# A hybrid decoder trunk on one core: more of the recurrence's small products as 64x64 quadrants, and the finishing norm one level later

## The reference

```python
kk = heads(k * k_k)
kk = kk / maximum(sqrt(sum(kk * kk, -1)), 1e-12)      # the key norm
k = k * (1.0 + (a - 1.0) * k_a)
def step(S, inp):
    sa = einsum('bhij,bhj->bhi', S, -kk_t)
    S = (S * w_t[:, :, None, :] + sa[..., :, None] * (kk_t * a_t)[:, :, None, :]
         + v_t[..., :, None] * k_t[..., None, :])
    return S, einsum('bhij,bhj->bhi', S, r_t)
y = (y - mean(y)) * rsqrt(var(y) + eps)               # the finishing norm, per head
y = y * ln_g + ln_b
bonus = sum(heads(r * k * r_k), -1) * heads(v)
return (y + bonus) * g
```

## Time and profile before

| | |
|---|---|
| median of 3 runs | 883.57 us (883.24 to 883.83) |
| profiled execution | 883.92 us, its span 882.1 us |
| mean granted TensorE clock | 0.977 |
| PE / PEld busy | 828.9 us (94%) / 555.5 us |
| DVE / ACT / POOL busy | 459.1 / 240.3 / 277.6 us |
| matmuls | 7071 records |

### The profile page before, as it was taken

One profiled execution on the slowest core, in us unless ns is written; L12 is line 12 of the kernel. 1 busy time (PEld: TensorE's weight loads), 2 busy tenths in 40 slices (PEclk: granted clock), 3 DMA queues, 4 the chain that ended last, 5 costly groups with the idle time before them and its releaser, 6 DMA issues.

```text
span 882.1 us, 17139 instructions
## 1 busy us (share of the span) xinstructions
PE 828.9 (94%) x7071; PEld 555.5 (63%) x7071; DVE 459.1 (52%) x1151; ACT 240.3 (27%) x581; POOL 277.6 (31%) x265
## 2 busy tenths in 40 slices
PE   4999999999999999899999999999999999999950
PEld 4656644454444445778887555555788888888830
DVE  3830468888731135676674234443655454555534
ACT  5420021111200132554543131222232232323214
POOL 4820000000399601542623000000044656534232
PEclk9999999999999999998999999999999999999995
DMA  9933443355201022100000692112889998998639
GB/s 335 293 83 109 155 137 124 119 158 161 63 25 47 25 72 93 55 4 3 4 4 4 225 378 88 49 48 87 313 315 292 304 301 268 281 264 260 200 68 368
DMA packets 79638, 136.34 MB, mean 155 GB/s; under 512 B 17133, under 2 KB 51146, under 8 KB 79562
## 3 DMA queue, kind: packets, MB, share of 16 engines
q1 hardware_dynamic: 69258, 118.44, 38.9%
q0 software_dynamic: 10304, 16.82, 8.0%
HBM read 124.18 MB, written 29.92 MB: 175 GB/s over the span
## 4 chain that ended last, share of the span: by engine, by line
PE 79%; DVE 10%; DMA 4%; issue 3%; ACT 1%; POOL 1%; SPq 0%; DVEq 0%; POOLq 0%; ACTq 0%
PE bank L781 74%; PE bank L1336 3%; DVE REG_Y L1655 3%; DMA REG_Y<-in_x 2%; DMA REG_Y<-xn_d,tbl 1%; DVE REG_P L2209 1%; DMA REG_P<-y_d 1%; ACT REG_W L1384 1%; PE bank L1267 1%; DVE REG_W L1765 1%; DVE mx L1768 1%; DMA y_d<-REG_Y,idx 1%; POOL y_d L718 1%; PE bank L1035 0%; DVE REG_W L1807 0%
## 5 line engine op out<-in xcount | busy, mean ns | idle before, releaser
L781 PE MATMUL bank<-REG_W 128*128 128x512 f32 (+2 forms) x832 | 275.8, 501 | 0.0
L781 PEld LDWEIGHTS bank<-REG_W 128*128 128x128 f32 (+1 forms) x832 | 126.6, 183 | 136.3 <-issue 135.2
L781 PE MATMUL bank<-REG_W,REG_Y 128*128 128x512 f32 x256 | 118.3, 599 | 1.4 <-DVE REG_Y L2164 1.1
L1384 ACT ACTIVATE REG_P<-bank 128x256 f32<-128x256 f32 (+2 forms) x126 | 53.4, 462 | 159.0 <-PE bank L781 136.7
L781 PE MATMUL bank<-REG_P 64*64 64x64 f32 (+3 forms) x2880 | 79.9, 231 | 5.9 <-issue 3.9
L781 PEld LDWEIGHTS bank<-REG_P 64*64 64x64 f32 (+1 forms) x2880 | 68.6, 139 | 16.1 <-issue 9.0
L1384 ACT ACTIVATE REG_Y<-bank,mod,s 128x128 f32<-128x128 f32 x136 | 51.1, 456 | 86.1 <-PE bank L1336 86.1
L781 PEld LDWEIGHTS bank<-REG_W,REG_Y 128*128 128x128 f32 x256 | 45.6, 191 | 44.3 <-issue 44.2
L781 PEld LDWEIGHTS bank<-REG_Y,REG_P 128*128 128x128 f32 (+1 forms) x616 | 63.2, 181 | 6.5 <-issue 6.5
L781 PE MATMUL bank<-REG_Y,REG_P 128*128 128x128 f32 (+1 forms) x616 | 66.5, 276 | 0.0
L625 POOL TENSOR_TENSOR REG_P<-REG_P 128x1040 f32<-128x1040 f32 x2 | 4.8, 2386 | 179.3 <-DVE REG_P L1744 179.2
(11 more groups left out here) (290 smaller groups left out, 1116.6 us busy)
## 6 DMA issues: line engine op xcount, KB each, us to landing
REG_P<-in_w_ada SPq DMA_DIRECT2D x18, 1024.0 KB, 6.3
REG_W<-in_w_in SPq DMA_DIRECT2D x17, 512.0 KB
REG_P<-in_moe_w_gate SPq DMA_DIRECT2D x17, 512.0 KB, 8.1
REG_W<-in_moe_w_gate SPq DMA_DIRECT2D x16, 512.0 KB, 6.3
REG_W<-in_moe_w_up SPq DMA_DIRECT2D x16, 512.0 KB, 9.3
REG_W<-in_moe_w_down SPq DMA_DIRECT2D x16, 512.0 KB, 14.4
REG_P<-in_moe_w_up SPq DMA_DIRECT2D x14, 512.0 KB, 13.8
REG_P<-in_w_ada SPq DMA_DIRECT2D x3, 2048.0 KB, 12.6
```

Source lines behind the costliest of these rows:

```text
L781: return pe.matmul(o_, l, r, start=start, stop=stop, skip_group_check=True)
L1384: return act.activation(o_, i_, f, **kw)
```

## The change

Everything is in the recurrence; POOL's turn is unchanged but for the width of a tile.

- V's centring (four products over 128x128) becomes 16 quadrants in banks 2 and 3; the turned keys (four transposes) become 16 quadrant products with the small identity. Both wait for ACT's evictions of bt and kt. ACT reads each over two banks (halves), and takes the turned keys behind the two small copies of xx.
- turn_sums, turn_flip and turn_back take the place of norm_sums, norm_flip and norm_back inside the turns, in banks 4 to 7: 16 quadrants with one column each, 4, and 8 with 128 columns. sel gets a second copy of its rows in the lower half, nrp is 64 wide and zeroed at the start, nrT has 128 rows.
- The finishing norm: sums from level 1 to level 2 (behind the W1 products), flip from between the halves of level 3 to behind them, spreading from ahead of level 4 to behind it. The key norm's sums go from between the halves of level 4 to behind them, its flip behind the uz products. The beside products at level 4 (two each in turns 1 and 2, three in turn 3) are gone.
- The bonus product (two over 128x128) becomes four diagonal quadrants in bank 5.

```diff
             def router_bias(k0, k1):
                 pe.wait_ge(s["mod2_ready"], 8)
+                pe.wait_ge(s["w_nbu"], tail_norm(TURNS - 2))
...
-                wait("w_tka", 4, 1)
+                wait("w_tka", 4, 2)
                 for n in range(2):
                     for p in range(2):
-                        t0 = PAD + m * W2 + n * P
-                        last = mm(PS[2][:, (2 * n + p) * P:(2 * n + p + 1) * P], pT[:, B_V + p, t0:t0 + P], cen[:, :])
-                last.then_inc(s["w_tok"], 1)
-                wait("w_tka", 4, 2)
-                flip_in(3, lambda p, tk: KR[:, p, 0, tk], 0)
+                        at = (2 * n + p) * HD
+                        for h, c in corners:
+                            t0 = PAD + m * W2 + n * P + CH * c
+                            last = mm(PS[2 + h][cr(c), at:at + HD], pT[hb(h), B_V + p, t0:t0 + CH], cen[hb(h), 64 * h:64 * h + 64])
...
+                        for h, c in corners:
+                            last = mm(PS[2 + h][cr(c), at:at + HD], KR[hb(h), p, 0, n * P + CH * c:n * P + CH * c + CH],
+                                      identq[hb(h), :])
...
-                    if tail and l == 4:
-                        if more:
-                            wait("w_gg", 1, 2)
-                        else:
-                            pe.wait_ge(s["w_tha"], TURNS)
-                            beside(3, 7)
-                        norm_back(tail_norm(m - 1))
...
-                    if tail and l == 3:
-                        norm_flip(tail_norm(m - 1))
                     if l == 1:
-                        if tail:
-                            norm_sums(tail_norm(m - 1), sqt, tail_squares(m - 1))
                         wait("w_tka", 4, 4)
-                    if more and l == 4:
-                        if tail:
-                            pe.wait_ge(s["w_nrT"], tail_norm(m - 1))
-                            beside(2, 4)
-                        norm_sums(front_norm(m + 1), sq, front_squares(m + 1))
+                    if l == 2:
+                        pe.wait_ge(s["w_tha"], min(m + 2, TURNS))
+                        pe.wait_ge(s["w_gg"], min(m + 2, TURNS))
+                    if tail and l == 2:
+                        turn_sums(tail_norm(m - 1), sqt, tail_squares(m - 1))
...
+                    if tail and l == 3:
+                        wait("w_w1", 1, 1)
+                        turn_flip(tail_norm(m - 1))
+                    if l == 4:
+                        if tail:
+                            pe.wait_ge(s["w_nrT"], tail_norm(m - 1))
+                        if more:
+                            turn_sums(front_norm(m + 1), sq, front_squares(m + 1))
+                        if tail:
+                            turn_back(tail_norm(m - 1))
...
                 for p in range(2):
-                    last = mm(PS[7][:, p * W2:(p + 1) * W2], brk[:, p, :], rk[:, p, :])
-                last.then_inc(s["w_bonp"], 1)
+                    for h in range(2):
+                        last = mm(PS[5][hb(h), p * W2:(p + 1) * W2], brk[hb(h), p, 64 * h:64 * h + 64], rk[hb(h), p, :])
...
+            corners = ((0, 0), (1, 1), (1, 0), (0, 1))
+            def turn_sums(k, squares, count):
+                pe.wait_ge(s["w_sq"], count)
+                pe.wait_ge(s["w_nrT"], k - 1)
+                for n in range(2):
+                    for p in range(2):
+                        at = 256 + n * 2 + p
+                        for h, c in corners:
+                            last = mm(PS[4 + h][cr(c), at:at + 1], squares[hb(h), p, n * P + CH * c:n * P + CH * c + CH],
+                                      ones[hb(h), 0:1])
...
+            def turn_flip(k):
+                pe.wait_ge(s["w_nrp"], k)
+                for c, g in corners:
+                    last = mm(PS[6 + c][hb(g), P:P + CH], nrp[cr(c), :], identq[cr(c), :])
...
+            def turn_back(k):
+                pe.wait_ge(s["w_nrT"], k)
+                pe.wait_ge(s["w_nbu"], k - 1)
+                for p in range(2):
+                    for n, h in corners:
+                        last = mm(PS[6 + n][hb(h), p * W2:p * W2 + P], sel[cr(n), n * 2 + p, 64 * h:64 * h + 64], nrT[cr(n), :])
```

More of the change, by code:

```diff
@@ L122, in sem @@
             return ctx.enter_context(nc.semaphore(name))
-        PS = [ctx.enter_context(nc.psum_tensor(f"bank{i}", [P, 512], F32)) for i in range(8)]
+        banks = ctx.enter_context(nc.psum_tensor("banks", [P, 8, 512], F32))
+        PS = [banks[:, i, :] for i in range(8)]
         xn2_d = nc.dram_tensor("xn2_d", [T, D], F32, kind="Internal")
@@ L1028, in norm_back @@
                     for n in range(2):
-                        last = mm(PS[5][:, p * W2 + n * P:p * W2 + (n + 1) * P], sel[:, n * 2 + p, :], nrT[:, :])
+                        last = mm(PS[5][:, p * W2 + n * P:p * W2 + (n + 1) * P], sel[0:8, n * 2 + p, :], nrT[0:8, :])
                 last.then_inc(s["w_nrb"], 1)
+            corners = ((0, 0), (1, 1), (1, 0), (0, 1))
+            def turn_sums(k, squares, count):
+                pe.wait_ge(s["w_sq"], count)
+                pe.wait_ge(s["w_nrT"], k - 1)
+                for n in range(2):
+                    for p in range(2):
[3 more added lines that the diff above has]
+                                      ones[hb(h), 0:1])
+                            if n == 1 and p == 1 and (h, c) in corners[2:]:
+                                last.then_inc(s["w_ss"], 1)
+            def turn_flip(k):
+                pe.wait_ge(s["w_nrp"], k)
+                for c, g in corners:
+                    last = mm(PS[6 + c][hb(g), P:P + CH], nrp[cr(c), :], identq[cr(c), :])
+                    if (c, g) in corners[2:]:
+                        last.then_inc(s["w_nrt"], 1)
+            def turn_back(k):
[4 more added lines that the diff above has]
+                        last = mm(PS[6 + n][hb(h), p * W2:p * W2 + P], sel[cr(n), n * 2 + p, 64 * h:64 * h + 64], nrT[cr(n), :])
+                        if p == 1 and (n, h) in corners[2:]:
+                            last.then_inc(s["w_nrb"], 1)
             def flip_in(bank, src, count):
@@ L1155, in turn @@
                     blocks(n, n, xT, lambda i, r: wk[r, i].rearrange("p a d -> p (a d)"), "w_uzp", P)
+                if more:
+                    if tail:
+                        pe.wait_ge(s["w_nbu"], tail_norm(m - 1))
+                    turn_flip(front_norm(m + 1))
                 pe.wait_ge(s["w_tha"], min(m + 2, TURNS))
                 for p in range(2):
-                    last = mm(PS[7][:, p * W2:(p + 1) * W2], brk[:, p, :], rk[:, p, :])
-                last.then_inc(s["w_bonp"], 1)
+                    for h in range(2):
+                        last = mm(PS[5][hb(h), p * W2:(p + 1) * W2], brk[hb(h), p, 64 * h:64 * h + 64], rk[hb(h), p, :])
+                        if p == 1:
+                            last.then_inc(s["w_bonp"], 1)
                 wait("w_uz", 2, 2)
@@ L1174, in turn @@
                 if more:
-                    norm_back(front_norm(m + 1))
+                    turn_back(front_norm(m + 1))
                 for n in range(2):
@@ L1870, in norm_turned, with back, by_half @@
             def norm_turned(k):
-                dve.wait_ge(s["w_nrt"], k)
-                dve.tensor_copy(nrT[:, :], PS[4][0:8, P:2 * P]).then_inc(s["w_nrT"], 1)
+                if k in (front_norm(0), tail_norm(TURNS - 1)):
+                    dve.wait_ge(s["w_nrt"], 1 if k == front_norm(0) else 2 * k - 2)
+                    dve.tensor_copy(nrT[0:8, :], PS[4][0:8, P:2 * P]).then_inc(s["w_nrT"], 1)
+                    return
+                dve.wait_ge(s["w_nrt"], 2 * k - 1)
+                dve.tensor_copy(nrT[:, :].rearrange("p (c t) -> p c t", c=2), banks[:, 6:8, P:P + CH]).then_inc(s["w_nrT"], 1)
+            def back(k):
+                if k in (front_norm(0), tail_norm(TURNS - 1)):
+                    dve.wait_ge(s["w_nrb"], 1 if k == front_norm(0) else 2 * k - 2)
+                    return PS[5][:, :].rearrange("p (a n t) -> p a n t", a=2, n=2)
+                dve.wait_ge(s["w_nrb"], 2 * k - 1)
+                return banks[:, 6:8, :].rearrange("p n (a x) -> p a n x", a=2)[:, :, :, 0:P]
+            def by_half(ap):
+                return ap.rearrange("p a (n t) -> p a n t", n=2)
             def log_decays(m, part=None):
@@ L1956, in turn @@
                         log_decays(m + 1, l - 1)
-                    if tail and l == 3:
+                    if tail and l == 4:
                         norm_turned(tail_norm(m - 1))
-                    if more and l == 4:
+                    if more and l == 5:
                         key_norm(m + 1)
```

59 lines of the change are left out of this document (35 added, 24 removed).

## The result

The kernel after took 888.46 us (median of 20 runs, 884.87 to 891.23), the kernel before, run beside it, 883.21 (20 runs, 876.83 to 887.87). The ratio is 1.0073 [1.0055, 1.0091]: 5 us slower where 5.6 us faster were forecast. The profiled execution of after took 889.05 us, its span is 887.3. First the page, then the stages (columns as in the earlier trace rows: length, busy time and count of PE, PEld, DVE, ACT, POOL, granted clock, DMA share, GB/s).

The account below looks back on a forecast made before the run. TensorE, busy 94% of the span, was taken as the bound, recurrence gains carrying through one for one. Turn gains of 7.4 us less 1.8 for instruction stops gave 5.6, from 883.9 to 878.3 us; range 874.0 to 884.5.

Parts of the forecast that it names:

- Instruction stops: TensorE idles in dense 64x64 work, read as late instruction blocks: 1.4 us returns plus 0.4 for more records, 1.8 us lost.
- my 7.4 us of gain: Recurrence, before subtracting instruction stops: 1.2 from turn 0, 3.9 from turn 1, 0.5 from turn 2, 1.8 from turn 3.
- Corner price: 64x64 records going round all four corners in the recurrence: 0.0153 us each, against 0.121 for 128-wide records.
- Rival C: Corners of one column or alternating tiles cost 0.0316 us a record; 10 us, half hidden under waits: 883.3 us; chance 0.08.
- POOL's order: Turns 1 to 3: the power stays ahead of mask 3, so TensorE stands about 2 us before level 3.
- The stop is paid back: Turn 2, level 4: 2.45 us of wide work goes, offsetting POOL's stop; level 5 starts about 438.7, before 438.55.
- The clock: Turn 1: the 6.9 us stretch at the 1.2 GHz level from 398.5 us goes, gaining 2.9 us.
- rival B: POOL's stop at level 3 drops the clock in each of turns 1, 2 and 3, 2.9 us each: 887.0; chance 0.12.
- Level 1: Turn 2: starts at 424.4 after POOL's first mask, not 424.86, 0.45 us gained; second half starts 426.07 instead of 426.92.
- End of the turn: Turn 2: bonus gives 0.15 us, norm_back 0.65; DVE's G and re then hold the last group by 0.2.
- Turn 0: No finishing norm, so no stop for POOL; level 4, flip, bonus and norm_back changes gain 1.2 us.

Follow-up runs that it names:

- mask_first: The kernel after, with POOL's finishing-norm power moved behind the mask of level 3; 883.45 us, ratio to before 0.9992.
- doubled: The kernel before, with 56 unread corner products added in each turn, 28 each ahead of the squares of levels 2 and 3; 896.71 us, ratio 1.0145.
- dense_alone: The kernel before, with 512 unread corner products on ready operands added near 20 us; 917.01 us in one run.
- stop_filled: The kernel after, with eight unread 128x128 products ahead of level 3 in turns 1 to 3; 888.25 us, ratio to before 1.0056.
- shifted: The kernel before, with 32 unread corner products (128 TensorE instructions) added near 20 us; 883.61 us, ratio 1.0024.
- late_mask: The kernel before, with the finishing norm a level later, key norm's sums behind level 4, 128 wide, and POOL's mask 3 ahead of the power; 888.9 us, ratio 1.0079.
- wide_instead: The kernel before, with 7 unread 128x128 products added in each turn ahead of the squares of levels 2 and 3; 882.98 us, ratio 1.0016.

## Why the prediction was wrong

**The step that failed is the term "Instruction stops".** It read the stops rightly as blocks that land late (all but the 0.53 us ahead of turn 1's spreading, which DVE's nrT ended), then scaled the sum of their lengths (12% more of 3.9 us, and 1.4 that return: 1.8). That is the wrong scaling. The visible stops are only the part of the supply's limit that no other wait hides; each wait that the change removes makes room for a stop. Counted in the traces, the recurrence's stops of over 0.2 us at ends of blocks are 5.6 us in before, 9.0 in after, 13.0 in mask_first and 12.4 in doubled. The price goes by block. In mask_first's turn 1 seven blocks in a row, from 382.8 to 410.5 us, took 3.7 to 4.2 us each; the dense ones of before's turn 0 took 3.5 to 4.0. The recurrence has 7,580 TensorE instructions in the trace of before and 8,478 in after's: 898/256 = 3.5 blocks, 12 to 15 us if all lay in dense stretches. mask_first tests the sum: my 7.4 us of gain and the 5.0 that POOL's order was worth make 12.4, and it measured 0.7 [-1.8, +3.3] under before. The missing 12 us are what the supply would take near its ceiling. mask_first's trace shows 7.4 of them there (13.0 - 5.6). Another 1.1 is POOL at level 4 of turn 1, and the 2.9 that I had put on turn 1's clock did not come, since it fell there again. One execution of each kernel stands behind this division, so it is rough.

Point by point, the rest:

- **Corner price.** Right by itself (16 and 17 ns in two rows of 32), wrong in use: doubled paid 29 to 31 ns. Rival C had 31.6 ns, from identq's two-corner blocks and so for another reason, and halved it as half hidden: 883.3. The Trainium skill ("TensorE: Matmul & The Clock Gate", Back-to-back issue gap) gives about 25 ns a matmul and would have made it 884, no change. No stretch of a single block bears that figure out (15.3 ns); in steady flow dense_alone shows 31.
- **POOL's order.** Place and mechanism right, in each of turns 1 to 3; the size off. The power took 2.48 us beside DVE's scan in turns 1 and 2. The stops were 3.3, 1.7 (behind an instruction stop of 1.4) and 2.4 us, where I had 2.2, 2.2 and 2.0. mask_first values the order at 5.0 us, the clock's falls that went with it included.
- **"The stop is paid back" at level 4.** Wrong. Level 4 did lose its 2.45 us of wide work, but an instruction stop of 1.57 us stood in the spreading. With the stop ahead of level 3 before it, level 5 started at 442.4, 22.4 us into the turn, against my 438.7, 19.6 into it.
- **The clock.** I expected turn 1's fall to go. It fell in each of turns 1 to 3, as rival B says, and in turn 0 too. Rival B's sign was right, its price was not: it had 2.9 us for each fall, and stop_filled puts all four at about 1.8. At 1.2 GHz after's dense records cost 3.40/100 = 34 ns against the supply's 31. A fall among wide work costs more: before's in turn 1 lasted 6.8 us, and shifted, without it, was 2.8 us shorter. In late_mask, where wide work stood in the low stretches, a fall may well have cost its half. Taken at the full clock, after's recurrence would be about 144.8 us and before's (shifted) is 139.4, so the loss does not go away with the falls.
- **Level 1.** Right. It starts 5.33 us into turn 2, where it was 5.78: 0.45 gained, as forecast, and it follows POOL's mask, which ended at 425.21. Its second half starts 0.7 us sooner, where I had 0.85, behind the idle of 0.76 for DVE's t1, which `keys_scaled` held up.
- **End of the turn.** G and re held the last group by 0.9, 0.9 and 0.8 us, not 0.2. Beside POOL's scalings DVE's finishing took longer (L1994 1.64 us for 128x512), and it comes a level later.
- **Turn 0,** put 1.2 shorter, became 1.8 longer: it has no finishing norm, so POOL has no part in this; 191 more instructions are 0.75 of a block, about 3 us. Nor is it the fall there: stop_filled's turn 0, at the full clock, took 36.1 us, after's 36.3.

## What to carry to other kernels

Before you cut a wide fp32 product into corners, count instructions as well as array time: four corners take four times the instructions, and where TensorE's stream is dense, the count sets the time. Look for "issue" idles whose distance is 128 load-and-matmul pairs; where they recur every 3.5 to 4 us, array work removed is worth little, and wide work added costs less than its array time (3.5 of 6.8 us here, at the same clock). When a step is moved a level later, write down for each queue it passes through what now stands ahead of what: here one instruction on POOL ahead of a mask was worth 5 us, and moving one of DVE's gained nothing because ACT's queue came next.

## What the runs showed of the hardware

- TensorE's instructions come in blocks of 256 (packets of 16,384 bytes). A steady run of ready 64x64 records used a block up in 1.96 us and got the next one 4.00 us after the last; this was the same in 48.27 to 52.27 us with the DMA engines at a share of 0.34 and in 52.27 to 56.27 with 0.89. With the share at 1.00 and above (340 GB/s and more, the two rows under dense_alone) blocks came 7.02 and 6.20 us apart.

```profile
48.27:52.27 4.00, 2.09 (x128) 1.96 (x128) 0.00 (x0) 0.00 (x0) 0.00 (x0) 1.00 0.34 37
52.27:56.27 4.00, 2.09 (x128) 1.96 (x128) 0.00 (x0) 0.00 (x0) 0.00 (x0) 1.00 0.89 189
```

- 448 extra corner records in dense levels cost 13 to 14 us. 56 records of 128x128 with the same array time cost 1.2 by the medians, and 3.5 between two profiled recurrences that both had the full clock.
- Executions of one kernel differ with the clock they were granted: of before's beside wide_instead, the shortest (876.59 us) had a mean of 0.986, the longest (884.82) 0.974.
- POOL's 128x8 power took 2.48 us beside DVE's scan, 1.64 to 1.75 otherwise.
